# Two stick-breaking steps moved into the second value product, and the later steps, rates and first pair products moved up with them

## What is computed

```python
h = rms_norm_2(x, norm_mix[l])
p = h @ w_in[l]
sb_q, sb_k, sb_v, rw_in = jnp.split(p, [SB_WIDTH, 2 * SB_WIDTH, 3 * SB_WIDTH], axis=-1)
...
z = jnp.einsum('bqhd,bkhd->bhqk', qb, kb).astype(jnp.float32) * scale
log_beta = jax.nn.log_sigmoid(z)
log_1m_beta = jnp.where(mask, jax.nn.log_sigmoid(-z), 0.0)
log_remain = lax.cumsum(log_1m_beta, axis=3, reverse=True) - log_1m_beta
att = jnp.where(mask, jnp.exp(log_beta + log_remain), 0.0)
outs.append(jnp.einsum('bhqk,bkhd->bqhd', att.astype(vb.dtype), vb))
...
u = u + (token_shift(u) - u) * mu
log_w = -jax.nn.softplus(-(w0 + jnp.tanh(x_w) @ w2)) - 0.5
decay = jnp.exp(-jnp.exp(log_w.astype(jnp.float32)))
a = jax.nn.sigmoid(a0 + x_a @ a2).astype(jnp.float32)
kk = kk / jnp.maximum(jnp.linalg.norm(kk, axis=-1, keepdims=True), 1e-12)
y = rwkv7_recurrence(r, heads(decay), kf, v, -kk, kk * a)
```

## Time and profile before

| what | value |
|---|---|
| runs before | 1955.57, 1956.26, 1958.94 us |
| the profiled execution | 1956.47 us |
| its span, first to last instruction | 1954.7 us |
| mean granted TensorE clock | 0.976 of full |
| TensorE busy | 1847.5 us, 95% |
| VectorE busy | 935.4 us, 48% |
| ScalarE busy | 697.1 us, 36% |
| POOL busy | 134.4 us, 7% |
| chain that ended last | TensorE 85%, VectorE 6%, ScalarE 3%, DMA 3% |

### The profile page before, as it was taken

How to read it: one execution, slowest core, us unless ns; L and a number is a source line. 1 busy time by engine, 2 the same in 40 slices (tenths; PEclk the granted TensorE clock), 3 DMA queues, 4 the chain that set the end, 5 groups by cost and what they waited for, 6 DMA issues and landing times.

```text
span 1954.7 us, 27696 instructions
## 1 busy us (share of the span) xinstructions
PE 1847.5 (95%) x11652; PEld 1425.1 (73%) x11652; DVE 935.4 (48%) x1482; ACT 697.1 (36%) x1055; POOL 134.4 (7%) x109
## 2 busy tenths in 40 slices
PE   5999988979999999999999999899888999999999
PEld 3666655758888887688888877666788688888887
DVE  4367766364343343544244444545754644423442
ACT  3225546343223233433123334577311432312221
POOL 0023434200000002000000010000000010000000
PEclk8999989989999999899999999999999899999999
DMA  9772100113222222123222322111000222322231
GB/s 374 257 253 74 37 25 33 55 43 99 96 97 97 97 97 88 64 97 117 78 91 100 111 67 85 55 43 44 23 4 4 66 96 97 112 82 87 97 124 38
DMA packets 44475, 176.15 MB, mean 90 GB/s; under 512 B 5568, under 2 KB 5824, under 8 KB 41024
## 3 DMA queue, kind: packets, MB, share of 16 engines
q1 hardware_dynamic: 44352, 174.38, 25.8%
HBM read 168.33 MB, written 2.10 MB: 87 GB/s over the span
## 4 chain that ended last, share of the span: by engine, by line
PE 85%; DVE 6%; ACT 3%; DMA 3%; issue 2%; SPq 0%; POOL 0%; DVEq 0%; ACTq 0%
PE bank L363 24%; PE bank L365 23%; PE bank L364 23%; PE bank L523 1%; PE bank L539 1%; PE bank L507 1%; DMA arena<-ada_late 1%; PE bank L712 1%; DMA arena<-ada 1%; PE bank L853 1%; ACT arena L1195 1%; PE bank L870 1%; PE bank L861 1%; DMA ring<-m_w_v 1%; DVE arena L2046 1%
## 5 line engine op out<-in xcount | busy, mean ns | idle before, releaser
L1557 DVE TENSOR_TENSOR wsp<-ring,wsp 128x1024 fp32r<-128x1024 f32 (+2 forms) x244 | 312.3, 1282 | 448.5 <-ACT wsp L1084 448.4
L363 PE MATMUL bank<-hs,wsp 128*128 128x512 f32 x1160 | 473.3, 408 | 15.7 <-DVE hs L1823 5.3
L1084 ACT ACTIVATE wsp<-ring 128x1024 fp32r<-128x1024 f32 (+2 forms) x244 | 268.8, 1104 | 599.5 <-PE bank L365 593.3
L365 PE MATMUL bank<-hs,wsp 128*128 128x512 f32 x1160 | 455.8, 393 | 0.0
L364 PE MATMUL bank<-hs,wsp 128*128 128x512 f32 x1160 | 455.5, 393 | 0.0
L363 PEld LDWEIGHTS bank<-hs,wsp 128*128 128x128 f32 x1160 | 220.0, 190 | 87.5 <-issue 32.0
L364 PEld LDWEIGHTS bank<-hs,wsp 128*128 128x128 f32 x1160 | 220.2, 190 | 50.2 <-issue 6.0
L365 PEld LDWEIGHTS bank<-hs,wsp 128*128 128x128 f32 x1160 | 219.7, 189 | 47.4
L365 PE MATMUL bank<-hids,wsp 128*128 128x512 f32 x608 | 241.0, 396 | 0.0
L364 PE MATMUL bank<-hids,wsp 128*128 128x512 f32 x608 | 241.0, 396 | 0.0
L363 PE MATMUL bank<-hids,wsp 128*128 128x512 f32 x608 | 241.0, 396 | 0.0
(11 more groups left out here) (340 smaller groups left out, 2103.8 us busy)
## 6 DMA issues: line engine op xcount, KB each, us to landing
ring<-m_gate SPq DMA_DIRECT2D x44, 512.0 KB, 3.4
ring<-m_up SPq DMA_DIRECT2D x44, 512.0 KB, 3.4
ring<-m_down SPq DMA_DIRECT2D x32, 704.0 KB, 4.0
ring<-m_w_in SPq DMA_DIRECT2D x38, 512.0 KB, 3.4
arena<-ada_late SPq DMA_DIRECT2D x16, 1024.0 KB, 7.1
ring<-m_w_up SPq DMA_DIRECT2D x32, 512.0 KB, 3.4
ring<-m_w_down SPq DMA_DIRECT2D x32, 512.0 KB, 3.4
ring<-m_w_out SPq DMA_DIRECT2D x16, 512.0 KB, 3.6
```

What stands on the lines that cost most here:

```text
L363: pe.matmul(out, lhs[0], rhs[0], start=start, stop=False)
L365: return pe.matmul(out, lhs[1], rhs[0], start=False, stop=stop)
L1084: act.activation(wsp[:, s % SPLIT, 0, 0:size], ring[:, i % RING, 0:size], ACT.Copy)\
L1557: dve.tensor_tensor(wsp[:, s % SPLIT, 1, 0:size], ring[:, i % RING, 0:size], wsp[:, s % SPLIT, 0, 0:size].bitcast(F32), ALU.subtract).then ...
```

## The change

It moves instructions and adds and removes none of them.

- On TensorE the scores of step 0 stand behind quarter 2 of the value product, and step 1 behind quarter 3. Step m + 1 stands where step m stood, behind products 4, 9 and so on, so step 13 ends behind product 59 and not 64.
- On ScalarE the logs of step 0 stand behind quarter 3's wait, ahead of pieces 4 and 5; step 1 stands ahead of the first two value copies.
- On VectorE mask 0 stands ahead of the low part of piece 4, softplus 0 ahead of that of piece 5, and step 1 ahead of that of piece 6.
- The rates go from tile 8 to tile 7: `rates(0)` and `rates(1)` behind product 0, `rates(2)` behind product 2, `rates(3)` behind product 4. `osb_ms(3)` follows behind product 6.
- Scan, keys and `decayed` of each c come one tile sooner. The four key norms are spread: norm c now stands between scan c and `keys(c)`.
- `first_products(c)` follows tile 10 + c and not 11 + c.

The core of the diff (TensorE, then ScalarE, then VectorE):

```diff
+            def beside_values(j):
+                if j == 0:
+                    head_norm(7)
+                if j == 1:
+                    pe.wait_ge(S("qk2"), 8)
+                    sb_step(0)
+                if j == 2:
+                    sb_step(1)
+
+            token_gemm("w_v2", 4, 2, T, "vtok2_full", "vtok2", VBANKS, beside_values)
...
-                    if (8 * n + k) % 5 == 4 and 8 * n + k < 5 * (PARTS + 1):
-                        sb_step((8 * n + k + 1) // 5)
-                    if (n, k) == (8, 2):
+                    if (8 * n + k) % 5 == 4 and 8 * n + k < 5 * PARTS:
+                        sb_step((8 * n + k + 1) // 5 + 1)
+                    if (n, k) == (7, 0):
                         rates(0)
                         rates(1)
-                    if (n, k) == (8, 4):
+                    if (n, k) == (7, 2):
+                        rates(2)
+                    if (n, k) == (7, 4):
+                        rates(3)
+                    if (n, k) == (7, 6):
                         osb_ms(3)
-                    if (n, k) == (8, 6):
-                        rates(2)
-                        rates(3)
...
-                if n >= 11:
-                    first_products(n - 11)
+                if n >= 10:
+                    first_products(n - 10)
             turn_values(2)
             turn_values(3)
-            first_products(3)
```

```diff
+            def values_read(j):
+                if j < 3:
+                    ahead("w_v2", j)
+                    act.wait_ge(S("w_v2_part"), j + 1)
+                if j == 2:
+                    act.wait_ge(S("qk2"), 8)
+                    sb_step(0)
+                if j == 3:
+                    sb_step(1)
+                    act.wait_ge(S("vtok2_full"), NT)
+                    values(0)
+                    values(1)
...
-                    if (n, k) == (8, 1):
+                    if (n, k) == (7, 0):
                         act.wait_ge(S("shifted"), 5)
                         act.activation(u[0:DH, UWA, :], u[0:DH, UWA, :], ACT.Tanh).then_inc(S("tanh"), 1)
-                    if (n, k) == (8, 2):
                         rates(0)
                         rates(1)
                         key_line(0)
-                        key_line(1)
-                    if (n, k) == (8, 6):
+                    if (n, k) == (7, 2):
                         rates(2)
+                    if (n, k) == (7, 4):
                         rates(3)
                         act.wait_ge(S("shifted"), 6)
                         act.activation(u[:, UG, :], u[:, UG, :], ACT.Sigmoid).then_inc(S("wa"), 1)
                         log_exp_tables()
-                    if (n, k) == (9, 1):
                         decays(0)
+                        key_line(1)
+                    if (n, k) == (8, 0):
                         osb_root(3)
...
-                if 10 <= n < 13:
-                    decays(n - 9)
-                if 10 <= n < 12:
-                    key_line(n - 8)
+                if 8 <= n < 11:
+                    decays(n - 7)
+                if 8 <= n < 10:
+                    key_line(n - 6)
```

```diff
+            def values_read(k):
+                if k in (0, 2, 4):
+                    ahead("w_v2", k // 2)
+                if k == 4:
+                    sb_mask(0)
+                if k == 5:
+                    softplus(0)
+                if k == 6:
+                    sb_step(1)
...
-                if n == 8:
+                if n == 7:
                     dve.wait_ge(S("sb_pv"), PARTS)
-                    for c in range(4):
-                        dve.wait_ge(S("kk_root"), c + 1)
...
                     scan(0)
+                    key_norm(0)
                     keys(0)
                 ahead("w_in2", 8 + n, ("w_in2", 21))
                 token_mix(n)
...
-                if 8 <= n < 12:
-                    decayed(n - 8)
+                if 7 <= n < 11:
+                    decayed(n - 7)
                 if n == 8:
                     osb_norm(3)
-                if 8 <= n < 11:
-                    scan(n - 7)
-                    keys(n - 7)
+                if 7 <= n < 10:
+                    scan(n - 6)
+                    key_norm(n - 6)
+                    keys(n - 6)
```

More of the change, by code:

```diff
@@ L385, in gemms, with token_gemm @@
                         sumsq(sums, k)
-            def token_gemm(name, tiles, kc, width, full, freed, at=(0, 1, 2, 3)):
+            def token_gemm(name, tiles, kc, width, full, freed, at=(0, 1, 2, 3), inside=None):
                 for t in range(NT):
@@ L406, in token_gemm @@
                         late_piece(j)
-                    if name == "w_v2" and j == 0:
-                        head_norm(7)
+                    if inside:
+                        inside(j)
             def sumsq(tag, k):
@@ L1384, in rates @@
                 if c == 0:
[L1385 removed]
                     act.wait_ge(S("sb_suffix"), PARTS)
+                if c >= 2:
+                    act.wait_ge(S("osb_normed"), 2 * c - 3)
                 act.wait_ge(S("wa_full"), 2 * c + 1)
@@ L1409, in turned_values, with values @@
                                ACT.Copy).then_inc(S("vtk"), 1)
-            sb_step(0)
+            def values(t):
+                act.activation(vtok2[:, t, :], bank[:, VBANKS[t], :], ACT.Identity, scale=rtok[:, t:t + 1]).then_inc(S("vtok2"), 1)
+                own("vtok2")
+            def values_read(j):
[10 more added lines that the diff above has]
+                    values(1)
+            norm_high("u")
+            values(2)
+            values(3)
+            ahead("w_v2", 3)
             for n in range(14):
                 for k in range(KD):
-                    if (8 * n + k) % 5 == 4 and 8 * n + k < 5 * (PARTS + 1):
-                        sb_step((8 * n + k + 1) // 5)
-                    if (n, k) == (8, 1):
+                    if (8 * n + k) % 5 == 4 and 8 * n + k < 5 * PARTS:
+                        sb_step((8 * n + k + 1) // 5 + 1)
+                    if (n, k) == (7, 0):
                         act.wait_ge(S("shifted"), 5)
                         act.activation(u[0:DH, UWA, :], u[0:DH, UWA, :], ACT.Tanh).then_inc(S("tanh"), 1)
-                    if (n, k) == (8, 2):
                         rates(0)
@@ L1910, in _ @@
                 own("qk2")
-            def values_read(k):
-                if k in (0, 2, 4):
-                    ahead("w_v2", k // 2)
-            normalize("u", lambda k: vec("norm_mix_2", k), root=rmix, read=values_read)
-            ahead("w_v2", 3)
             def sb_mask(p):
@@ L1982, in scan, with key_norm @@
                 own("csum")
+            def key_norm(c):
+                dve.wait_ge(S("kk_root"), c + 1)
+                dve.scalar_tensor_tensor(out=knorm[:, c, :], in0=u[:, UK + c, :], scalar=vec("rw_k_k", c),
+                                         in1=u[:, UV + c, :], op0=ALU.mult, op1=ALU.mult).then_inc(S("knorm"), 1)
+                own("knorm")
             def keys(c):
@@ L2011, in bonus @@
                 dve.tensor_tensor(u[:, UV + c, :], bank[:, 6 + c % 2, :], u[:, UV + c, :], ALU.mult).then_inc(S("bonus"), 1)
-            sb_step(0)
+            def values_read(k):
[7 more added lines that the diff above has]
+                    sb_step(1)
+            normalize("u", lambda k: vec("norm_mix_2", k), root=rmix, read=values_read)
+            ahead("w_v2", 3)
             for n in range(14):
                 for k in range(KD):
-                    if (8 * n + k) % 5 == 4 and 8 * n + k < 5 * (PARTS + 1):
-                        sb_step((8 * n + k + 1) // 5)
-                if n == 8:
+                    if (8 * n + k) % 5 == 4 and 8 * n + k < 5 * PARTS:
+                        sb_step((8 * n + k + 1) // 5 + 1)
+                if n == 7:
                     dve.wait_ge(S("sb_pv"), PARTS)
-                    for c in range(4):
-                        dve.wait_ge(S("kk_root"), c + 1)
-                        dve.scalar_tensor_tensor(out=knorm[:, c, :], in0=u[:, UK + c, :], scalar=vec("rw_k_k", c),
-                                                 in1=u[:, UV + c, :], op0=ALU.mult, op1=ALU.mult).then_inc(S("knorm"), 1)
-                        own("knorm")
                     scan(0)
+                    key_norm(0)
                     keys(0)
```

20 lines of the change are left out of this document (removed).

## The result

| | median of its runs, us | profiled execution, us | its span | granted clock |
|---|---|---|---|---|
| before | 1955.91 (10 runs beside the change) | 1956.47 | 1954.7 | 0.976 |
| changed | 1967.33 (10 runs) | 1965.94 | 1964.2 | 0.977 |

A forecast was written before the change was run, and what follows sets the result against it. TensorE, 95% busy, was taken to bound the kernel, other engines costing time only where it waits. Early 2.9 us plus late 7.3 us gave 10.2 us on a median of 1956.26, so 1966.5 us, range 1958.5 to 1970.0.

The forecast's parts named there:

- Part 1: First two steps inside the value product: suffix product waits 7.8 us instead of 5.4, clock drops again; costs 2.9 us.
- Part 2: Steps 2 to 13, five products sooner: TensorE covers them with no wait of note, so no cost.
- Cost nothing: Claim for steps 2 to 13, from walking all queues from tile 2 to tile 6: five products sooner adds no time.
- Part 3: Rates a tile sooner: TensorE waits 4.9 us for tanh instead of 1.7, with a clock drop costing 0.9 + 0.3 us.
- VectorE's chain: VectorE's late low parts, shifts, decayed, scans, norms and keys; forecast to begin 20.6 us after tile 6's end, before 22.8.
- Part 4: Late tiles: VectorE sets them; shift 10 ends 50.4 us after tile 6 instead of 42.1, so loop ends 7.8 us later.
- charged drop: Clock drop charged to each lengthened wait, at suffix product and tanh; without either, the sum would be 3.1 us smaller.
- Sum: Whole change: 2.9 us early plus 7.3 us late, 10.2 us slower, with ends of 7.1 and 12.1 us.
- upper bound of 12.1: Upper end of the total: the drop after the 7.8 us suffix wait lasts twice as long, another 1.9 us.
- Faster: Rival: work moves into idle time, VectorE's chain starts by 10.7 us after tile 6's end, 1950.8 us; chance 0.07.
- Nothing measurable: Rival: ScalarE's backlog at tile 6's end is smaller, tanh waits only 1.7 us, 1960.2 us; chance 0.11.

The follow-up runs named there:

- Logs ahead: Changed kernel with ScalarE's logs of step 0 ahead of the split waiting for quarter 3, VectorE's mask and softplus earlier; ratio to before 1.0048.
- early alone: Changed kernel with rates, key norms, scans, keys, decayed and first products back in their tiles of before; ratio to before 1.0019.
- Rates four products later: Changed kernel with TensorE running four more products of tile 7 ahead of the rates, other queues as changed; ratio to before 1.0034.
- logs ahead, late part as before: Changed kernel with step 0's logs, mask and softplus earlier, and rates, norms, scans, keys, decayed, first products in their places of before; ratio to before 0.9992.
- spread rates: Against "logs ahead, late part as before": tanh at tile 7's head, TensorE's rates from tile 7 product 6 into tile 8, norms at tile 7; ratio to before 0.9976.

## Why the prediction was right, and where its terms were off

The sign, the mechanism and the size hold: 1967.33 us against 1966.5, inside the range. That the two agree to 0.8 us is luck: the stretch itself lost 13.7 us where the sum had 10.2, and the runs cannot tell the two.

**Part 1** was right. Wait 7.84 us (forecast 7.8), clock drop of 3.8 us, step 2 done at 1257.0 on the clock of before (1258.25 less the 1.25 by which this execution is later; forecast 1256.8). "Logs ahead" shows the cause: take logs and softplus out from behind split, copy and pieces, and the wait is 0.7 us. The scores of steps 0 and 1 start 10.9 and 8.8 us sooner than before (1225.28 and 1231.80, less 1.25, against 1234.91 and 1239.39). The split that stands ahead of mask and logs comes 8.2 us sooner (1231.97, less 1.25, against 1238.94), and the suffix product only 6.4 (1240.56, less 1.25, against 1245.73).

**Part 2** was wrong by one term. "Cost nothing" had walked products and parts, but not bank 7: the head sums for key norm 2 now come right behind those for output norm 1 and must wait for ScalarE to read that bank. That is 1.3 us, shown by moving it. With it the early part and the steps should cost 4.2; early alone measured 4.6, and 0.4 us is not assigned.

**Part 3** had the right chain and too small a term. The tanh wait was 4.95 us (4.9), but VectorE's chain began 22.3 us after tile 6's end (1366.02 - 1343.70), not 20.6. ScalarE waited 2.2, 0.6 and 0.7 us for rates and a value product from TensorE, which was itself slow behind the drop; I had charged 1.2 us for all of that. ScalarE's rows with these waits, VectorE's row with which its chain begins, and the window behind the wait for tanh:

```profile
1351.66 1.28 ACT L1377 ACT_TABLE_LOAD   x1 [2.21 <-PE bank L760]
...
1358.02 0.60 ACT L1341 ACTIVATE tmp<-bank 128x512 f32<-128x512 f32 x1 [0.59 <-PE bank L730]
...
1360.01 0.69 ACT L1377 ACTIVATE arena<-bank,col 128x512 f32<-128x512 f32 x1 [0.73 <-PE bank L760]
```

```profile
1366.02 1.23 DVE L1566 TENSOR_TENSOR wsp<-ring,wsp 128x1024 fp32r<-128x1024 f32 x1 [3.73 <-ACT wsp L1091]
```

```profile
1349.50:1353.20 3.70, 3.69 (x8) 1.19 (x8) 0.00 (x0) 1.52 (x2) 0.00 (x0) 0.50 0.03 13
```

"Rates four products later" gave back 2.7 us by this path.

**Part 4** was right for its own length: from the chain's start to the end of shift 10 it forecast 29.8 us and 29.9 came (52.2 - 22.3). Tile 13 starts at 58.9, 36.6 us after the chain's start (forecast 36.5). The split into waits was not: 3.1, 2.0 and 1.2 us came for 2.7, 3.8 and 1.4, because drops of the clock stretched the tiles between them, at no cost, as forecast.

**The clock.** A drop was charged to each wait longer than those that had one before. Where it was charged it came: 0.50 behind the 7.84 us, in all five kernels with that wait, and 0.50 behind the 4.95 us. That a charged drop could be absent in a given run was my own reading, and none of these executions had it so. Nor does a wait's length alone decide, as the other kernels show: "logs ahead, late part as before" waited 3.33 us for a shift and ran the next 6.2 us at 1.00, then waited 2.06 us and ran the next 6.4 us at 0.73.

**Sum.** Locally 13.7 us, 10.2 forecast. The bank gives 1.3 of the difference, the later chain start 1.7, and 0.5 stays open. The upper bound of 12.1 was too low for the stretch, though not for the median: the runs' interval of 8.4 to 16.4 us holds both numbers.

**The rivals.** "Faster" needed VectorE's chain to start at 10.7; it started at 22.3. "Nothing measurable" needed a tanh wait of 1.7 us; it was 4.95. The spread rates show that the first was a matter of place: with TensorE's rates behind ScalarE's tanh, and the norms in VectorE's idle time, moving this work is worth 3.1 us of the stretch.

That matmuls keep their order, by which the forecast let quarter 4 stand behind the waiting suffix product, is what the trace has: quarter 4 starts at 1243.99, behind both suffix products. The page "TensorE: Matmul & The Clock Gate" of the Trainium skill says in its section "Part 2: What happens when you issue a matmul", under "Step-by-step: what each phase is for", that only weight loads are pulled ahead and matmuls stay in order; the trace agrees.

## What to carry to other kernels

Moving a step earlier on one engine moves the wait, unless every instruction that feeds it is also moved past what stands ahead of it in its own queue. Here the scores came 9 to 11 us sooner, but mask, logs and softplus still stood behind a split that waits for the quarter itself. Before filling an engine's idle time, follow the chain that ended last through the tight stretch behind it: work is cheap only where that chain's engine idles, not where the mean busy share is 50%. And walk every shared buffer, also the small sums between two large pieces.

## What the hardware did that was not expected

- A shorter wait left a longer slow stretch, in the one execution of that kernel that was profiled. Behind 7.84 us of waiting the clock was 0.50 for 3.8 us; behind 6.07 us it was 0.50 for 4.2 us and 0.92 in the 6.6 us after. Of 1.8 us saved, 0.7 went there. From the suffix product to tile 0 it took 9.9 to 10.1 us in the five kernels that waited 7.84 us, and 10.8 in the one that waited 6.07. Whether the wait's length or chance made this is open. The same page of the Trainium skill, section "Part 1: The HAM clock gate", says that the number of slow matmuls varies from run to run; a spread of 0.2 us over five kernels shows little of that here.
- Where a drop falls decides what it costs. The same instructions between shifts 11 and 12 took 4.21 us in the changed kernel and 5.54 with the logs ahead. In the first the clock had been low in tile 11, under VectorE's cover; in the second it fell in tile 12, without cover. A gain of 2.45 us shrank to 1.0 in this way.
- No drop followed waits of 1.0, 1.24 and 1.7 us. After waits of 3.1 us there was one, with mean clocks of 0.73 in 6.4 us (changed) and 0.72 in 6.0 (logs ahead). But it also came behind shorter waits, 2.0 us at tile 11 (changed, 0.62 in 3.1 us) and 2.06 at tile 12 (logs ahead, late part as before), and did not come behind 3.33 us in that last kernel. So the length of the wait alone does not decide; what does is open.
- Runs of one kernel on one core differ by 11 us (before, 1949.52 to 1960.30) and 17 us (changed, 1958.85 to 1975.56), about as much as the whole effect here. In the two profiled executions compared, 5.5 us of it lay in a stretch that the change does not touch.
